# The pool's means moved ahead of a small add on VectorE, and the second post-norm gate's preparation spread into the stages before and after it

## What is computed

```python
def multiscale_pool(v, pool_w, pool_scale, on_grid):      # layer 0, windows 2, 4, 8, 16
    for gi, w in enumerate(POOL_WINDOWS):
        vg = v[..., gi * POOL_GROUP:(gi + 1) * POOL_GROUP]
        m = box_mean(...)                                  # rows, then columns; or one axis
        outs.append(m - vg)
    mixed = einsum('bngi,gio->bngo', pooled, pool_w) * pool_scale

shift, scale, gate = jnp.split(s_lat @ ada_w[layer] + ada_b[layer], 3)
h = rms_norm(x, pre_g[layer]) * (1.0 + scale) + shift
# layer 1 projects h and runs 16 heads of chunked scans to y
x = x + gate * rms_norm(y, post_g[layer])

ang = positions[..., None] * inv_freq                      # second block
cos, sin = jnp.cos(ang), jnp.sin(ang)
```

## Time and profile before

| | us |
|---|---|
| median of 3 runs | 2828.7 (2828.06 to 2832.36) |
| the profiled execution | 2829.58 |
| its span | 2827.4 |
| PE busy | 2682.7 (95%) |
| DVE busy | 1899.8 (67%) |
| ACT busy | 1273.1 (45%) |
| mean granted clock of TensorE | 0.983 |

### The profile page before, as it was taken

One profiled execution on the slowest core, in us unless ns is written; L12 is line 12 of the kernel. 1 busy time (PEld: TensorE's weight loads), 2 busy tenths in 40 slices (PEclk: granted clock), 3 DMA queues, 4 the chain that ended last, 5 costly groups with the idle time before them and its releaser, 6 DMA issues.

```text
span 2827.4 us, 36465 instructions
## 1 busy us (share of the span) xinstructions
PE 2682.7 (95%) x13605; PEld 2209.7 (78%) x13605; DVE 1899.8 (67%) x2677; ACT 1273.1 (45%) x2016; POOL 0.2 (0%) x4
## 2 busy tenths in 40 slices
PE   5998899999999989999999999988999989999988
PEld 2576678888778878888888888777878777878867
DVE  5755567877888567767767767856656555656654
ACT  6653222122322644534444445546455645544553
POOL 0000000000000000000000000000000000000000
PEclk9999999999999999999999999999999999999989
DMA  8763456655465433333333333454644455544453
GB/s 310 267 217 128 132 152 191 206 162 178 171 217 199 146 90 91 101 111 93 101 103 102 93 102 102 141 186 150 190 140 151 147 208 177 170 149 149 150 178 134
DMA packets 406588, 437.16 MB, mean 155 GB/s; under 512 B 22718, under 2 KB 286536, under 8 KB 404936
## 3 DMA queue, kind: packets, MB, share of 16 engines
q1 hardware_dynamic: 397760, 408.99, 45.3%
q10 hardware_dynamic: 8712, 26.59, 2.6%
HBM read 427.14 MB, written 8.39 MB: 154 GB/s over the span
## 4 chain that ended last, share of the span: by engine, by line
PE 81%; DVE 10%; ACT 5%; issue 2%; DMA 1%; ACTq 0%; DVEq 0%; SPq 0%
PE ps L1118 14%; PE ps L1119 14%; PE ps L1120 14%; PE ps L1121 9%; PE ps L1123 9%; PE ps L1122 9%; DVE wl L1779 3%; DVE acc L1850 2%; ACT wh L577 1%; PE ps L1428 1%; PE ps L1142 1%; PE ps L1449 1%; PE ps L1144 1%; PE ps L1433 1%; PE ps L1720 1%
## 5 line engine op out<-in xcount | busy, mean ns | idle before, releaser
L1779 DVE TENSOR_TENSOR wl<-raw,wh 128x1024 fp32r<-128x1024 f32 (+2 forms) x784 | 822.0, 1079 | 477.5 <-ACT wh L577 466.2
L577 ACT ACTIVATE wh<-raw 128x1024 fp32r<-128x1024 f32 (+2 forms) x784 | 714.3, 943 | 853.3 <-PE ps L1120 493.7
L1118 PE MATMUL ps<-hTh,wh 128*128 128x512 f32 (+1 forms) x2124 | 783.7, 369 | 38.1 <-DVE wl L1779 28.4
L1119 PE MATMUL ps<-hTl,wh 128*128 128x512 f32 (+1 forms) x2124 | 772.0, 363 | 0.0
L1120 PE MATMUL ps<-hTh,wl 128*128 128x512 f32 (+1 forms) x2124 | 770.1, 363 | 0.0
L1121 PE MATMUL ps<-wh,hTh 128*128 128x512 f32 (+1 forms) x1440 | 577.5, 401 | 26.9 <-DVE wl L1779 18.5
L1123 PE MATMUL ps<-wh,hTl 128*128 128x512 f32 (+1 forms) x1440 | 559.9, 389 | 0.0
L1122 PE MATMUL ps<-wl,hTh 128*128 128x512 f32 (+1 forms) x1440 | 559.5, 389 | 0.0
L1118 PEld LDWEIGHTS ps<-hTh,wh 128*128 128x128 f32 x2124 | 405.4, 191 | 110.3 <-DVE wl L1779 29.6
L1119 PEld LDWEIGHTS ps<-hTl,wh 128*128 128x128 f32 x2124 | 405.1, 191 | 62.4 <-issue 0.5
L1120 PEld LDWEIGHTS ps<-hTh,wl 128*128 128x128 f32 x2124 | 404.5, 190 | 63.0
(11 more groups left out here) (295 smaller groups left out, 2029.3 us busy)
## 6 DMA issues: line engine op xcount, KB each, us to landing
raw<-in_ada_w_dram SPq DMA_DIRECT2D x96, 1024.0 KB, 5.2
raw<-in_w_in_dram SPq DMA_DIRECT2D x88, 1024.0 KB, 5.1
raw<-in_od_w_in_dram SPq DMA_DIRECT2D x256, 320.0 KB, 3.5
raw<-in_ev_w_in_dram SPq DMA_DIRECT2D x192, 256.0 KB, 3.9
raw<-in_w_out_dram SPq DMA_DIRECT2D x32, 1024.0 KB, 5.1
raw<-in_ev_w_out_dram SPq DMA_DIRECT2D x16, 1024.0 KB, 5.2
raw<-in_od_w_out_dram SPq DMA_DIRECT2D x16, 1024.0 KB, 5.1
x_save<-arena ACTq DMA_DIRECT2D x6, 1024.0 KB, 5.4
```

What stands on the lines that cost most here:

```text
L577: nc.scalar.activation(wh[:, ch.spl, part], raw[:, ch.raw, part], ACT.Copy).then_inc(s_hi, 1)
L1118: nc.tensor.matmul(out, w_h, x_h, start=first, stop=False, skip_group_check=True)
L1119: nc.tensor.matmul(out, w_h, x_l, start=False, stop=False, skip_group_check=True)
L1779: nc.vector.tensor_tensor(wl[:, ch.spl, part], raw[:, ch.raw, part], wh[:, ch.spl, part].bitcast(F32), ALU.subtract).then_inc(s_lo, 1)
```

## The change

Three edits go together. In the diff, the first `head` with `moved` is ACT's, the second with `between` alone is DVE's; the body of the angles' instructions is unchanged and becomes `angles()`.

1. In the pool passes and in the first convolution block, `pool_means` stands ahead of `ada_columns` on DVE.
2. The second gate's diagonals 8 to 11 get a buffer each, in the columns of `raw` that the heads' weights leave free (`SIDE`), and DVE makes them in head 0: `gate_scale(1)`, 8 and 9 after the units of chunk 3, 10 and 11 after those of chunk 4. The wait for `gate_rows(r - 1)` goes. ACT keeps `spread` 8 and 9 in their place, then makes the high part of head 1's chunk 0 and loads the table of exp by a one-column instruction; `spread` 10 and 11 follow the copies from head 0's banks, ahead of chunk 1.
3. DVE makes the angles inside `head(1)`, between `lo` of chunk 0 and `gates(0)`; ACT takes the sines after chunk 4 of `head(1)`; PE's wait for the angles moves from chunk 1 to chunk 3; DVE's wait for the sines moves to their first use, in the second block.

```diff
         def gate_block(r):
-            return dg[:, :, :] if r >= 8 else X4[...]
+            return SIDE[:, r - 8, :, :].rearrange("p t (a b) -> p t a b", a=2) if r >= 8 else X4[...]
...
+                if moved:
+                    moved()
                 split(1)
...
                 split(4)
+                if between:
+                    between()
...
-            for q in range(4):
+            for q in range(2):
                 spread(8 + q, q, 0, GB1)
-
-            act.wait_ge(s_ang, 1)
-            nc.scalar.activation(csn, csn, ACT.Sin).then_inc(s_sin, 1)
+            hi(st.chunk("hg", 1, 0), 10 * P)
+            step(nc.scalar.activation(small[:, 506:507], eps, ACT.Exp)).done()
...
-            head(1, head_chunks(1), fin=False)
+            head(1, lambda c: head_chunks(1)(c) if c else None, fin=False, moved=last_spreads, between=sines)
...
                 if c == 1:
                     pe.wait_ge(s_gbe, 12)
+                if c == 3:
                     pe.wait_ge(s_ang, 1)
...
                     if i == 3:
+                        pool_means(g - 1, POOL_WINDOWS[g - 1])
                         ada_columns(7 + g, 7 + g)
-                        pool_means(g - 1, POOL_WINDOWS[g - 1])
...
             def gate_diag(r):
-                if r > 8:
-                    dve.wait_ge(s_gb, r)
...
                     low_unit(2 * c + 3)
+                if c == 3:
+                    dve.wait_ge(s_qT, 6)
+                    gate_scale(1)
+                if c in (3, 4):
+                    gate_diag(2 * c + 2)
+                    gate_diag(2 * c + 3)
...
-            dve.wait_ge(s_qT, 6)
-            gate_scale(1)
-            for r in range(8, 12):
-                gate_diag(r)
-
             dve.wait_ge(s_pos, 16)
             nc.vector.tensor_copy(posr, posi).then_inc(s_posf, 1)
...
-            dve.wait_ge(s_sin, 1)
...
                 split(0)
+                if between:
+                    between()
...
-            head(1, head_chunks(1), fin=False)
+            head(1, head_chunks(1), fin=False, between=angles)
...
+                if L == 0:
+                    dve.wait_ge(s_sin, 1)
```

More of the change, by code:

```diff
@@ L451, in gate_block @@
         def gate_block(r):
-            return dg[:, :, :] if r >= 8 else X4[:, r % 4, (2 + r // 4) * BLK:(3 + r // 4) * BLK].rearrange("p (a b) -> p a b", a=4)
+            return SIDE[:, r - 8, :, :].rearrange("p t (a b) -> p t a b", a=2) if r >= 8 else X4[:, r % 4, (2 + r // 4) * BLK:(3 + r // 4) * BLK].rearrange("p (a b) -> p a b", a=4)
         def x_turned(t, j):
@@ L826, in _, with head @@
                     unit(2 * c + 3)
-            def head(h, split, comp=True, fin=True):
+            def head(h, split, comp=True, fin=True, moved=None, between=None):
                 split(0)
@@ L888, in _, with sines, last_spreads @@
             act.dma_start(posi, a["positions_2"][0].rearrange("(t p) -> t p", t=2)).then_inc(s_pos, 16)
-            for q in range(4):
+            for q in range(2):
                 spread(8 + q, q, 0, GB1)
-            act.wait_ge(s_ang, 1)
-            nc.scalar.activation(csn, csn, ACT.Sin).then_inc(s_sin, 1)
+            hi(st.chunk("hg", 1, 0), 10 * P)
+            step(nc.scalar.activation(small[:, 506:507], eps, ACT.Exp)).done()
+            def sines():
+                act.wait_ge(s_ang, 1)
+                nc.scalar.activation(csn, csn, ACT.Sin).then_inc(s_sin, 1)
             act.wait_ge(s_save, 32)
             act.wait_ge(s_plo, 2 * KT)
-            head(1, head_chunks(1), fin=False)
+            def last_spreads():
+                for q in range(2, 4):
+                    spread(8 + q, q, 0, GB1)
+            head(1, lambda c: head_chunks(1)(c) if c else None, fin=False, moved=last_spreads, between=sines)
             with act.Fori(2, HEADS) as h, step.loop(h, 2, HEADS - 2, 1):
@@ L2041, in _ @@
             lo(st.chunk("conv", 0, 2))
+            pool_means(3, POOL_WINDOWS[3])
             ada_columns(11, 11)
-            pool_means(3, POOL_WINDOWS[3])
             ada_products(0, 0)
@@ L2079, in gate_diag @@
                 q, v = r % 4, r // 4 % 2
-                if r > 8:
-                    dve.wait_ge(s_gb, r)
-                nc.vector.tensor_tensor(gate_block(r), ident.unsqueeze(1).broadcast_to([P, 4, P]),
-                                        gp[:, 4 * q:4 * q + 4, v].unsqueeze(2).broadcast_to([P, 4, P]), ALU.mult).then_inc(s_gd, 1)
+                four = lambda x: x.rearrange("p (a b) c -> p a b c", a=2) if r >= 8 else x
+                nc.vector.tensor_tensor(gate_block(r), four(ident.unsqueeze(1).broadcast_to([P, 4, P])),
+                                        four(gp[:, 4 * q:4 * q + 4, v].unsqueeze(2).broadcast_to([P, 4, P])), ALU.mult).then_inc(s_gd, 1)
             lo(out0(0))
@@ L2219, in _, with angles @@
-            step(nc.vector.scalar_tensor_tensor(out=turns_, in0=ang, scalar=-1.0, in1=ang, op0=ALU.mult, op1=ALU.max)).done()
-            nc.vector.tensor_scalar(csn[:, 0:64], turns_, -1.0, 1.5707963267948966, ALU.mult, ALU.add).then_inc(s_ang, 1)
-            dve.wait_ge(s_sin, 1)
+            def angles():
+                dve.wait_ge(s_posT, 1)
+                step(nc.vector.tensor_copy(posf, ps[:, 5, 0:2])).done()
+                for t in range(2):
+                    step(nc.vector.tensor_scalar(ang[:, 32 * t:32 * t + 32], C("invf"), posf[:, t:t + 1], None, ALU.mult))
+                step.done()
+                step(nc.vector.tensor_scalar(turns_, ang, 1.0 / TWO_PI, ROUND, ALU.mult, ALU.add)).done()
+                step(nc.vector.tensor_scalar(turns_, turns_, -ROUND, None, ALU.add)).done()
+                for piece in (PI_HI, PI_MID, PI_LO):
+                    step(nc.vector.scalar_tensor_tensor(out=ang, in0=turns_, scalar=-piece, in1=ang, op0=ALU.mult, op1=ALU.add)).done()
+                step(nc.vector.tensor_scalar(ang, ang, 3.1415925, -3.1415925, ALU.min, ALU.max)).done()
+                step(nc.vector.scalar_tensor_tensor(out=turns_, in0=ang, scalar=-1.0, in1=ang, op0=ALU.mult, op1=ALU.max)).done()
+                nc.vector.tensor_scalar(csn[:, 0:64], turns_, -1.0, 1.5707963267948966, ALU.mult, ALU.add).then_inc(s_ang, 1)
@@ L2222, in _, with head @@
             dve.wait_ge(s_save, 32)
             chunked = lambda x: x.rearrange("p (n c) -> p n c", c=CHUNK)
-            def head(h, split, comp=True, fin=True):
+            def head(h, split, comp=True, fin=True, between=None):
                 def bound(x, d):
```

## The result

The changed kernel takes 2794.9 us, median of 4 runs (2791.23 to 2796.17), where the kernel before takes 2828.4 beside it (2827.09 to 2832.36). The ratio is 0.9877, with a 95% interval from 0.986 to 0.9894: 1.2% faster. The forecast was 2799.2, range 2794 to 2806. The median lies near the range's low end, and the gain was 33.5 us where 29.5 were forecast. The profiled execution took 2791.23.

What follows compares the result with a forecast made beforehand. PE bounds the kernel (81% of the chain), standing idle in the pool passes and between the heads. 21.5 + 8.0 = 29.5 us off the profiled 2829.6 gives 2800.1, median 0.9 lower: 2799.2, range 2794 to 2806.

Steps and rivals of the forecast that it cites:

- three stops and three slow stretches: Pool passes: PE's stops for chunk 4's low half and the slow clock behind them go, 5.5 + 7.5 + 8.5 = 21.5 us.
- The spares of 0.4 us at the passes and 0.3 in head 0: Chunk 4's low half comes just before PE needs it, by 0.4 us in the passes and 0.3 in head 0.
- The one ahead of the scan: Head 1: ACT's Ln, delayed by the sines, still ends 0.8 us ahead of DVE's scan.
- by the nearest row, 1.87, I take the price: 1.7 us: Head 1, ahead of chunk 1: the new 1.8 us stop also slows the clock, 1.7 us, bounds 0 and 1.9.
- the heads' term: Head 0 to head 1: chunk 1 begins 9.7 us earlier, less 1.7 for the slow clock, net 8.0 us.
- the new stop stays warm: Rival, head 1: no slow clock behind the stop ahead of chunk 1, so 2797.5 us; chance 0.28.
- Thin covers failing: Rival: chunk 4's covers in passes or head 0 fail, or table switches cost 2.7 us; 2802 to 2805, chance 0.15.
- The pool's gain given back to the loads: Rival, pool passes: DMA loads take back half the gain (2810 us) or all of it (2820.7); chance 0.06.
- The chain of reciprocals behind the angles: Rival, head 1: reciprocals start 2.6 us late in each direction, PE waits twice, 10 us in all; 2807, chance 0.05.
- Slower through the clock: Rival, head 1: the clock falls to half at the new stop and stays, losing over 29.5 + 5.7 us; chance 0.02.
- The drain behind a table load: Head 1, ACT: a skill page's 1.38 us drain per load would put Ln's end 2 us behind the scan.
- The positions' DMA: Head 0 to head 1: PE needs it 9 us later than its start; bounds 0 and 3 us, taken as 0.

Runs made afterwards that it cites:

- the two experiments that used them up: Changed kernel with every running-means sum made twice in the three passes: 2794.17 us; changed kernel with all four diagonals after chunk 3: 2793.65 us.
- The timed parts: Kernel before with only the means moved ahead of the add: 2802.62 us; changed kernel with only that move undone: 2814.93 us.
- the doubled means: Changed kernel with every sum of the pool's running means made twice in the three passes: 2794.17 us, ratio 0.9878.
- the faster version: Changed kernel with PE turning the positions before the last two gate spreads: 2789.28 us, ratio 0.9873; once more 2792.05, ratio 0.9866.
- the one of 3.43 us in an experiment: PE's stop in the changed kernel with the angles ahead of the low half of head 1's chunk 0: 2794.45 us, ratio 0.9881.
- the pool's part alone: Kernel before with only the means ahead of the add, in the passes and first convolution block: 2802.62 us, ratio 0.992.
- four loads in a row: Changed kernel with a one-column exp and sine behind head 1's sines, so ACT loads its table twice more: 2796.56 us, ratio 0.9884.

## Why the prediction came out as it did

**The mechanism was right, place by place.** The means behind the add were what held chunk 4's low half, and moving them took away three stops and three slow stretches: forecast 21.5, and 21.5 against the same profile that the forecast was read from (5.5, 7.5, 8.55). The spares of 0.4 us at the passes and 0.3 in head 0 held, and the two experiments that used them up paid what was left over. The one ahead of the scan was 0.4, not 0.8, and held too. The diagonals, the spreads and the emptying of the banks came as written: head 1's first chunk was forecast at 1002.4 in the old count and came within 0.2 us of it. The angles made one new stop; forecast 1.8 by the pace of issue, measured 1.6 (1.44 beyond the modelled end). Chunk 1 was forecast at 1010.1 and came at 1009.9 in the same count (986.59 plus the lead of 23.36).

**The step that failed is a price: "by the nearest row, 1.87, I take the price: 1.7 us".** I charged the slow clock to the new stop, so the heads' term was 8.0 where 9.9 were measured. The reading behind it was wrong, not only the value. One row each for 1.87 us (slow) and 2.06 us (not) was taken as a property of those stops; a third row of that trace, the 1.45 us stop at 943.29 with 0.64 behind it, was left out. Thirteen profiles show that the same 1.87 us stop was followed by a slow stretch in 5 and by none in 8, and the new stop by none in 7. The rival "the new stop stays warm" had it at 2797.5, 31.2 us; 31.4 were measured at the places of the edits.

**The same reading mis-sized the other terms too.** That price explains 1.9 of the 4.0 us between the gain forecast (29.5) and the one measured (33.5). The rest is about what the removed stops cost more in other executions: the slow stretches in 21.5 and in the heads' old stretch were read from one execution, which had the shortest ones. Three executions of the three stops give 21.5, 23.5 and 23.0, two of the heads' stretch 9.9 and 11.2; their means add up to 33.2. The timed parts gave 22.6 and 11.0. That 21.5 was met to a tenth is therefore partly luck of the comparison: forecast and check used the same profile of the kernel before.

**The range was too high at its low end for the same reason.** It allowed 1 us for rounding and spread. The clock behind stops that no edit touches moved the profiled executions by more: 1.6 of the 38.0 us at the convolution block's stop, and 4.8 between the heads' end and the last instruction. Three profiles of the same changed kernel have spans of 2789.4, 2785.0 and 2790.0. Timed runs have their mean granted clock on record as well, and it goes with their time: 0.985 in the fastest run of the kernel before beside the experiments (2821.7) and 0.981 in the slowest (2832.9), 0.991 in the changed kernel's fastest (2786.8) and 0.987 in its slowest (2797.4). The mean of those 31 runs of the kernel before is 2827.2, that of all 12 runs of the changed kernel 2793.9: 33.3 us. How a single execution comes by its slow stretches stays open.

**The rivals.** Thin covers failing: no, as above. The pool's gain given back to the loads: no, the leads of 5.7, 13.2 and 21.8 stay to the end. The chain of reciprocals behind the angles: no second stop in head 1. Slower through the clock: no slow stretch followed the new stop at all. The drain behind a table load: not there in any of the switches shown. The new stop stays warm: yes, and its forecast of 2797.5 is still 2.6 above the median, for the reason above.

## What to carry to other kernels

When an engine waits ahead of a short instruction and a long one that needs nothing new stands behind it, swap them: if the long one fits into the wait (7.1 us into 9.1 here), what is behind both comes earlier by its whole length; if it doesn't, what exceeds the wait is paid, as with the doubled means (1.7 us). A chain across engines that ends in a table load belongs behind work of the engine that it would stop, link by link; turn or load its input ahead of the last piece of independent work, as the faster version does. And price the slow clock behind a stop from several executions: for a new stop of 1 to 2 us it was a chance (5 of 13 at most, in these profiles) and belongs into the range; for the stops of 3.6 us and more that an edit removes it came each time, and in some executions up to 1.1 us longer than in others.

## What the runs showed that I had not expected

- The same stop, 1.87 us at the same matmul with the same work on both sides, left the granted clock at 1.00 in 8 profiles and let it fall (mean 0.64 over the next 4.8 us, 1.6 us lost) in 5. Stops of 3.62, 5.04 and 6.46 us, and the one of 3.43 us in an experiment, were followed by a slow stretch. Behind the one of 3.1 to 3.3 us at the last output block the mean clock of 4.8 us was under 0.7 in 11 profiles and 1.00 in 2.
- Waits of 1.12 and 0.8 us with two matmuls between them were enough once: with the pool's part alone the clock behind them was 0.64, in the kernel before 1.00.
- A table load on ScalarE occupied 1.28 us, and the instruction that needed it began 0.01 to 0.02 us later, also with four loads in a row.
- The positions' DMA of 1 KB released its cast 2.2 us after it was issued (969.91 to 972.15), 6.6 us ahead of PE's turn of them. The prediction had kept 0 to 3 us open for it; it cost nothing.
